# Attention weights two items ahead in second halves too, with scores for three items in the room of the eleventh gather slot

## What is computed

```python
def peer_ffn(xn, w_query, sub_keys, peer_u, peer_v):
    ...
    sk = jnp.einsum('thcd,ckd->thck', q, sub_keys).astype(jnp.float32)
    top_s, top_i = lax.top_k(sk, PEER_TOPK)
    ...
    best_s, best_pos = lax.top_k(cand_s, PEER_TOPK)
    idx = jnp.take_along_axis(cand_i, best_pos, axis=-1)
    gate = jax.nn.softmax(best_s, axis=-1)
    ...
        h = jnp.einsum('thkd,td->thk', peer_u[ib], xb).astype(jnp.float32)
        a = (gb * jax.nn.gelu(h, approximate=False)).astype(xb.dtype)
        return jnp.einsum('thk,thkd->td', a, peer_v[ib])
```

```python
    mx = jnp.maximum(jnp.max(sc, axis=-1, keepdims=True), sink)
    e = jnp.exp(sc - mx)
    pr = e / (jnp.sum(e, axis=-1, keepdims=True) + jnp.exp(sink - mx))
    ...
        a = jax.nn.softmax(sc, axis=-1)
        w = a[:, :, 0] - lam * a[:, :, 1]
```

## Time and profile before

| | us |
|---|---|
| median of 3 runs (2913.78 to 2915.91) | 2914.38 |
| the profiled execution | 2912.42 |
| its span, first to last instruction | 2910.6 |
| busy: PE, DVE, ACT, POOL | 2077.9, 2052.5, 1063.6, 1203.3 |
| mean granted TensorE clock | 0.850 |

### The profile page before, as it was taken

The page is one execution under the profiler, slowest core; times in us unless marked ns, Lnnn a source line. Parts: engine busy times, 40 slices in busy tenths (PEclk is TensorE's granted clock), DMA queues, the critical chain, the costliest instruction groups (busy, mean ns, idle before and its releaser), DMA issues.

```text
span 2910.6 us, 37403 instructions
## 1 busy us (share of the span) xinstructions
PE 2077.9 (71%) x12792; PEld 1031.8 (35%) x12792; DVE 2052.5 (71%) x5222; ACT 1063.6 (37%) x3372; POOL 1203.3 (41%) x1028
## 2 busy tenths in 40 slices
PE   8987887777868776677776877776776556555655
PEld 7644443344434432243442533224343111111111
DVE  3565678976667788866658678976657766677665
ACT  3432445623233456323224345633323222222222
POOL 0043343553344445444343444553444444444443
PEclk9998898888888888798887988888888776877687
DMA  6299999999999999999999999999999999999998
GB/s 236 105 422 420 421 421 397 406 419 419 421 421 420 421 421 414 417 421 421 421 420 382 421 421 421 421 418 421 421 420 418 420 419 417 419 418 416 417 417 333
DMA packets 162175, 1173.27 MB, mean 403 GB/s; under 512 B 17984, under 2 KB 18240, under 8 KB 19904
## 3 DMA queue, kind: packets, MB, share of 16 engines
q0 software_dynamic: 147456, 1073.81, 89.1%
q1 hardware_dynamic: 14528, 97.07, 8.2%
HBM read 1168.71 MB, written 2.10 MB: 402 GB/s over the span
## 4 chain that ended last, share of the span: by engine, by line
DMA 53%; PE 21%; DVE 18%; issue 4%; ACT 4%; POOL 0%; SPq 0%; DVEq 0%; POOLq 0%; ACTq 0%
DMA gather<-experts,idx 53%; PE ysum L810 10%; DVE gather L1513 9%; PE bank L533 7%; ACT amp L1089 2%; ACT diag L1097 1%; PE bank L584 1%; ACT gel L1082 1%; DVE shared L1242 1%; PE bank L610 1%; PE bank L555 1%; PE bank L779 1%; PE ysum L542 0%; DVE scratch L1438 0%; DVE scratch L1442 0%
## 5 line engine op out<-in xcount | busy, mean ns | idle before, releaser
L479 POOL DMA_INDIRECT gather<-experts,idx x1024 | 1203.1, 1175 | 1684.3 <-PE ysum L810 1323.2
L810 PE MATMUL ysum<-gather,diag 64*64 64x512 f32 x8192 | 1242.9, 758 | 717.0 <-ACT diag L1097 715.8
L1513 DVE CUSTOM_DVE_ANT_0 gather<-gather,xc 128x1024 f32<-128x1024 f32 x1024 | 1230.0, 1224 | 685.6 <-DMA gather<-experts,idx 647.6
L810 PEld LDWEIGHTS ysum<-gather,diag 64*64 64x64 f32 x8192 | 362.3, 170 | 1501.5 <-ACT diag L1097 925.9
L1082 ACT ACTIVATE gel<-hdot 128x4 f32<-128x4 f32 x255 | 52.4, 205 | 1588.8 <-DVE hdot L1513 1578.5
L533 PE MATMUL bank<-xnT,w 128*128 128x256 f32 (+1 forms) x2048 | 464.0, 382 | 11.2 <-DVE xnT L1167 11.2
L533 PEld LDWEIGHTS bank<-xnT,w 128*128 128x128 f32 x2048 | 377.8, 193 | 102.2 <-issue 40.8
L1097 ACT ACTIVATE diag<-cc,amp 128x64 f32<-128x64 f32 x1020 | 269.1, 333 | 8.6 <-PE ysum L810 4.4
L1089 ACT ACTIVATE amp<-gel,gate 128x1 f32<-128x1 f32 x1020 | 216.9, 283 | 8.4
L1082 ACT ACT_TABLE_LOAD x109 | 139.8, 1283 | 1.9
L779 PEld LDWEIGHTS bank<-w,yT 128*128 128x128 f32 x768 | 87.3, 192 | 17.4 <-issue 16.6
(11 more groups left out here) (151 smaller groups left out, 1486.2 us busy)
## 6 DMA issues: line engine op xcount, KB each, us to landing
w<-weights SPq DMA_DIRECT2D x82, 1024.0 KB
gather<-experts,idx POOLq DMA_INDIRECT x1024
gather<-weights SPq DMA_DIRECT2D x4, 1024.0 KB, 6.9
y_out<-x SPq DMA_DIRECT2D x4, 512.0 KB
x<-x_in SPq DMA_DIRECT2D x2, 512.0 KB, 4.4
g2b<-g_rows SPq DMA_DIRECT2D x2, 512.0 KB, 12.6
x<-x_in SPq DMA_DIRECT2D x1, 1024.0 KB, 13.3
cc<-consts_in SPq DMA_DIRECT2D x1, 856.0 KB, 11.0
```

What stands on the lines that cost most here:

```text
L479: pool.indirect_dma_start(gather[:, n % SLOTS, :], None, uv_d[m // 2], bass.IndirectOffsetOnAxis(ap=idx[:, g % 2, k:k + 1], axis=0)).then_ ...
L810: mm = nc.tensor.matmul(ysum[outs, q * 512:(q + 1) * 512], diag[toks, n % NDIAG, :], gather[toks, n % SLOTS, DM + hf * 512:DM + (hf + 1) * ...
L1513: e = V.tensor_tensor_reduce(out=gather[:, n % SLOTS, 0:DM], in0=gather[:, n % SLOTS, 0:DM], in1=xc[:, :], scale=1.0, scalar=0.0, op0=ALU. ...
```

## The change

Second halves hold the scores of three items. DVE makes the weights two items ahead of their turn, and ACT's exponential of item a + 2 moves from the end of slice a to its head. The copies in `pt` stay at two buffers (`TURNED`). The tile `shared` grows by 1024 floats a partition, and `gather` shrinks by one slot of 2048.

```diff
@@ -35,7 +35,7 @@
 HEADS, TOPK, NKEYS = 8, 16, 128
 CH = 4
 CHUNKS = HEADS * TT * TOPK // CH
-SLOTS = 11
+SLOTS = 10
 NDIAG = 4
 WS = 4
 BIG = 3.0e38
@@ -47,7 +47,8 @@
 ZP, ZH, ZG, ZC = (7, 8), (9, 12), (10, 13), (11, 14)
 NZ = 15
 NV = 3
-AHEAD = (4, 2)
+AHEAD = (4, 3)
+TURNED = (4, 2)
 
 Plan = namedtuple("Plan", "before z means conv pool squares sums")
 
@@ -232,10 +233,11 @@
         x = sb("x", SEQ // P, DM)
         gather = sb("gather", SLOTS, 2 * DM)
         xnT = sb("xnT", KD, HALF)
-        shared = sb("shared", 16 * HALF + 512)
+        shared = sb("shared", 16 * HALF + 1536)
         zt = shared[:, 0:10 * HALF].rearrange("p (i t) -> p i t", t=HALF)
 
-        sc = [shared[:, 10 * HALF:10 * HALF + 2048].rearrange("p (s m k) -> p s m k", s=n, m=2) for n in AHEAD]
+        sc = [shared[:, 10 * HALF:10 * HALF + 1024 * (2 + half)].rearrange("p (s m k) -> p s m k", s=n, m=2)
+              for half, n in enumerate(AHEAD)]
         qT = shared[:, 0:16 * HALF].rearrange("p (i t) -> p i t", t=HALF)
         kB = sb("kB", SEQ)
         kD = sb("kD", 2, SEQ)
@@ -257,7 +259,7 @@
         sq_y = xnT
         sd = sb("sd", 2, HALF)
         pt_all = sb("pt", 1024)
-        pt = [pt_all[:, :].rearrange("p (s k) -> p s k", s=n) for n in AHEAD]
+        pt = [pt_all[:, :].rearrange("p (s k) -> p s k", s=n) for n in TURNED]
         ss = sb("ss", 4)
         sdv = sb("sdv", 4)
         r1 = sb("r1", TT)
@@ -628,7 +630,7 @@
                 n = t + 1 - k0
                 for b in range(n):
                     mm = nc.tensor.matmul(ps[rows, 0:P], vAll[:, k0 + b, col:col + 64],
-                                          ptb[:, a % ahead, b * P:(b + 1) * P], start=b == 0, stop=b == n - 1)
+                                          ptb[:, a % TURNED[half], b * P:(b + 1) * P], start=b == 0, stop=b == n - 1)
                 mm.then_inc(s_ready, 1)
 
             def pool_product():
@@ -932,7 +934,7 @@
             def empty_turned(a):
                 swa, t, h, k0 = item(m, a)
                 cols = (t + 1 - k0) * P
-                empty(("t", a), ptb[:, a % ahead, 0:cols], bank_of(m, ("t", a))[:, 0:cols])
+                empty(("t", a), ptb[:, a % TURNED[half], 0:cols], bank_of(m, ("t", a))[:, 0:cols])
 
             def empty_out(a):
                 swa, t, h, k0 = item(m, a)
@@ -941,7 +943,7 @@
                       bank_of(m, ("o", a))[rows, 0:P])
 
             tile = [slice(t * P, (t + 1) * P) for t in range(TT)]
-            for a in range(ahead - 1 + half):
+            for a in range(ahead - 1):
                 attn_exp(a)
             for i in plan.before[1:]:
                 empty_z(i)
@@ -950,7 +952,7 @@
                 yield
             for a in range(ITEMS + 1 if m else plan.sums):
                 if a < ITEMS:
-                    if half == 0 and a + ahead - 1 < (ITEMS if m else 12):
+                    if a + ahead - 1 < (ITEMS if m else 12):
                         attn_exp(a + ahead - 1)
                     empty_turned(a)
                 if a:
@@ -965,9 +967,6 @@
                 if m:
                     if a == plan.sums:
                         root(("ys", 0), 3 * m + 1)
-                    if half and a + ahead < ITEMS:
-
-                        attn_exp(a + ahead)
                     yield
             if m:
                 root(("ys", 1), 3 * m + 2)
@@ -1325,8 +1324,7 @@
             if m:
                 yield
             attn_weights(0)
-            if half == 0:
-                attn_weights(1)
+            attn_weights(1)
             if m:
                 yield
             for a in range(ITEMS + 1 if m else plan.sums):
@@ -1340,9 +1338,9 @@
                     pool_tile(plan.means.index(a))
                 if a in plan.conv:
                     conv_tile(plan.conv.index(a))
-                if half and a + 1 < ITEMS:
-
-                    attn_weights(a + 1)
+                if half and a + 2 < ITEMS:
+
+                    attn_weights(a + 2)
                 if m:
                     if a == plan.sums + 1:
                         reciprocal_root(("ys", 0), 3 * m + 1)
```

## The result

The changed kernel took 2931.86 us (median of 4 runs, 2929.06 to 2935.16) against 2914.82 us for the kernel before beside it: a ratio of 1.0057, 95% interval 1.0046 to 1.0069. It is 17 us slower, nearly three times the 0.2% that a measurement can tell.

A forecast was written before the change was run, and what follows sets the result against it. The prediction took the gathers (DMA) to bound the kernel. Terms +2.0, +1.7 and +0.5 sum to +4.2 us on the profiled 2912.42, so 2916.6; the median being 2.0 above, 2918.6 us, range 2911 to 2926.

The forecast's parts named there:

- this attention: Second half's attention in the first block's experts: DVE's lateness and the missing slot cost +2.0 us, bounds -4 to +5.0.
- the other second half: Third block's experts: DVE falls some 7 us behind, mostly carried by the ring; +0.5 us, bounds 0 and 5.
- the slot elsewhere: Places where the ring is nearly empty, 702.33 us (1.2) and 1582 us (0.5): +1.7 us, bounds 0 and 5.
- my 15 to 35: Both second halves: DVE's new waits for ACT's exponentials were to total 15 to 35 us.
- my +3.3, +4.4 - 1.4 and -1.6: First block: DVE's waits at chunks 34 and 35, less the bias already done, and chunk 36's weights already done.
- the 2.74 us of chunk 29: First block, chunk 29: DVE's 2.74 us stand for the scores of item 10 was to go.
- Nearer to 2 than to 6: Dips around 500 us in the kernel before: real loss nearer 2 us than the 5.8 us of missing bytes.
- the first rival: First block's attention: DVE hardly waits, the 5.8 us of missing bytes return, less 1.7 for the slot: 2910.3 us; chance 0.12.
- The third rival: Slot missed at four or five long POOL silences, DVE's 7 us in the other second half reach DMA: 2926.4; chance 0.23.

The follow-up runs named there:

- again: The changed kernel unedited, measured once more beside the experiments: 2932.16 us, ratio 1.0063 against the kernel before.
- slot10: The kernel before with 10 gather slots in place of 11, nothing else changed: 2920.74 us, ratio 1.0023.
- slot9: The kernel before with 9 gather slots in place of 11: 2938.24 us, ratio 1.0084.
- wait11: The kernel before, 11 slots, scores for two items, with ACT's exponential moved into the slice of its weights: 2925.47 us, ratio 1.0037.
- order11: The changed kernel with 11 gather slots, the third item's scores laid over spent key scores: 2920.23 us, ratio 1.0020 against the kernel before.
- early10: The changed kernel, ten slots, with the exponential of item a+3 at the end of slice a: 2918.69 us, ratio 1.0015 against the kernel before.
- late11: order11, but in slice a DVE forms the weights of a+1, as in the kernel before: 2913.92 us, ratio 0.9999 against the kernel before.
- early11: The changed kernel with the edits of early10 and order11 together: 2913.58 us, ratio 0.9994 against the kernel before.
- busy11: early11 with useless DVE additions ahead of the weights where the changed kernel waits: 2928.51 us, ratio 1.0045 against the kernel before.

## Why the prediction was wrong

I said 2918.6 us, 2911 to 2926; it is 2931.9. One sign that I had asked for is missing: 490 to 510 us was to be above 380 GB/s and reads 379 and 331. And one that I had named as proof of being wrong is there, a dip between 1820 and 1900 us. These are windows of the changed kernel, and then the one of 1820 to 1900 us before and after:

```profile
490.00:500.00 10.00, 6.14 (x24) 2.71 (x28) 9.38 (x33) 7.44 (x20) 0.78 (x1) 0.50 0.91 379
500.00:510.00 10.00, 5.79 (x36) 1.62 (x32) 9.93 (x18) 2.02 (x9) 5.10 (x5) 0.67 0.90 331
```

```profile
1820.00:1900.00 80.00, 54.08 (x362) 21.75 (x360) 73.54 (x193) 51.63 (x135) 44.01 (x33) 0.89 1.01 421
1820.00:1900.00 80.00, 51.20 (x317) 20.44 (x317) 63.73 (x156) 47.80 (x121) 34.10 (x30) 0.83 0.97 390
```

To see where time was lost, take the start of a chunk's first dot product in the timeline of each run and subtract the kernel before's. The table has this lateness in us, first for chunks of the first block's experts, then of the third's, from one profiled execution each, so one or two microseconds in it say nothing.

| | chunk 20 | chunk 34 | chunk 37 | chunk 44 | third block, chunk 8 | third block, chunk 40 |
|---|---|---|---|---|---|---|
| start in the kernel before | 376.1 | 544.0 | 571.2 | 634.6 | 1655.1 | 1996.1 |
| changed kernel | 2.2 | 1.0 | 6.4 | 9.0 | 14.4 | 19.5 |
| again | 2.9 | 1.3 | 6.8 | 9.1 | 14.6 | 18.8 |
| slot10 | 0.1 | -0.2 | -0.1 | 2.2 | 6.7 | 5.2 |
| slot9 | 8.1 | 8.5 | 8.5 | 12.9 | 25.9 | 26.1 |
| wait11 | 2.0 | 2.1 | 10.2 | 10.7 | 10.8 | 14.8 |
| order11 | -0.1 | 0.2 | 5.6 | 6.1 | 4.4 | 7.8 |
| early10 | 3.5 | 1.3 | -1.7 | 3.3 | 7.7 | 6.7 |
| late11 | -1.7 | -0.5 | -1.7 | 0.2 | -0.4 | 0.1 |
| early11 | 1.1 | 0.6 | -2.4 | 1.4 | 1.3 | 1.6 |
| busy11 | 1.5 | 2.5 | 8.7 | 10.8 | 11.2 | 17.0 |

The mechanisms of the forecast were there, and all three terms of its sum were too small: this attention 2.0, measured 6.8 (chunk 20 to 44); the other second half 0.5, measured 5.1 (its chunk 8 to 40); the slot elsewhere 1.7, measured 5.4 between the two stretches and 2.2 up to chunk 20 (slot10 has 0.1 there, so the 2.2 are not safely the slot's).

**What came right.** 560 to 600 us was to be slower and is, and the waits of VectorE were found at their places and sizes. I had 3.3, 2.9, 2.6, 3.3 and 4.4 us in chunks 22, 23, 27, 34 and 35. The trace has 3.30, 2.96, 2.72, 3.51 and 4.60, out of the 0.01 us between table load and exponential that the row of before showed. The Trainium skill, ScalarE: Activation LUTs, section What ACT_TABLE_LOAD costs, adds a drain of 1380 ns to each switch. The trace disagrees: the load starts where the diagonals end, the exponential starts 0.02 us behind the load of 1.28 (562.97, then 564.27), and the waits fit without a drain. The total was 41.4 us, above my 15 to 35: from 1815 us on the third block has 14.6 us of waits where I had 12.6, but it has 9.4 us more in four waits before that, which I had not looked at. It also came right that the waits of chunks 22 to 27 are free: order11 stands 0.2 us late at chunk 34.

**The other second half, "+0.5", bounds 0 to 5: the step that failed by the largest factor.** The changed kernel lost 5.1 us there, ten times the term, and order11 3.4. I had VectorE 7 us behind by my own sum and let the ring carry that, because it had carried most of a silence of POOL of 17.93 us. But that was one silence behind a stretch with spare time. Here eight waits come within 260 us. The first four, up to 1806 us, cost no rate (421 GB/s from 1740 to 1820 us in both kernels). VectorE's waits from 1768 to 1932 us, of the kernel before and then of the changed one:

```profile
DVE gather L1513 <- DMA gather<-experts,idx: 14.8, 12, 3.4
```

```profile
DVE st L1263 <- ACT shared L915: 19.2, 6, 4.6
```

The changed kernel's VectorE has no wait for a gather left in these 164 us: its spare time there is used up, and at the last waits the rate falls (390 GB/s from 1820 to 1900 us). slot10 and early10 keep 418 GB/s in the window from 1810 to 1960 us and lose nothing between the two chunks of the table, order11 has 396. So the loss comes with the wait. Whether ten slots made it dearer (5.1 against 3.4 us) is not shown.

**This attention, "+2.0", bounds -4 to +5.** It lost 6.8 us, over its upper bound, and order11, with the slot in place, lost 6.2. I had VectorE 2.5 us late from chunk 36 on. order11 is 5.6 us late at chunk 37, and the way there can be followed. The waits of chunks 34 and 35 were paid as I had priced them (0.2 to 5.6 us; my +3.3, +4.4 - 1.4 and -1.6 make 4.7). What did not come is the gain ahead of them: by my sum VectorE was to be 2.2 us early at chunk 34. It came to chunk 29 1.2 us late (early11, without any of the waits, 1.4), was 1.7 us early at chunk 30, so the 2.74 us of chunk 29 did go, and lost that again in chunk 31, where its wait for scores grew from 3.2 to 4.67 us and I had +0.3. PE, too, was to be free 3.5 us earlier at chunk 29; it stands 7.91 us instead of 6.85, for a bank that the third item's scores need. I had read in the code that the six banks come in a fixed order, and had counted only the bank of item 10's scores. ScalarE's new order is the smaller part of that wait: early11, with the exponentials behind the copies, still has 6.70, and there ScalarE had stood 5.71 us for the chunk's dot products ahead of its copy. From chunk 37 to 44 the changed kernel loses 2.6 us more, about as slot10 does with 2.3, and order11 with its eleven slots 0.5: that is the slot.

**The slot elsewhere, "+1.7", bounds 0 to 5.** slot10 as a whole cost 7.1 us. At 700 us it lost 3.3 us more than before where I had 1.2, and 1.3 us in the window from 290 to 350, where I had nothing; at 1582 us, where I had 0.5, the stretch from 1560 to 1700 reads 401 GB/s in both. I had priced a slot as at most its own 2.49 us of transfer at a place; at 700 us the loss was more than that. In the table slot10, early10 and the changed kernel lose 4.5, 4.4 and 5.4 us between the two attention stretches, and order11, wait11 and early11 with their eleven slots nothing.

**"Nearer to 2 than to 6".** I held that the dips of before hid little loss. early11, which makes them shallower, gained 1.5 us with an interval that includes zero, so this stands as far as it was tested. From chunk 20 to 37 early11 gained 3.5 us on VectorE, and by chunk 44 nothing of it was left: VectorE waits for gathers again there, and they came no earlier. A gain as large as the first rival's was never there.

The third rival (2926.4, 0.23) had the mechanism nearest to what happened, the slot at several places and VectorE's lateness reaching DMA, and even its price was 5.5 us short. It had 5 us for the other second half, which is what was measured, and 5 for the slot's places; what it lacked is in this attention, where it kept my 2.0.

## What to carry to other kernels

When a consumer's step moves a slice earlier, move its producer's step too: here the exponential had stood a slice ahead of the weights, and keeping that distance gave back 12 of 17 us. Spare time covers a late step only at its own place: the four waits in chunks 22 to 27 fell on spare time and cost nothing, the two in chunks 34 and 35, 8.1 us, fell where there was none and left VectorE 5.4 us later. A forecast that sets a gain at one place against a wait at another must show that the gain is still there when the wait comes. The price of a slot in a ring of buffers was not a slope here: the eleventh slot was worth 7 us and the tenth 16. A slot given up for an optimisation is best priced by a run with one slot less, ahead of the optimisation.

## What the runs showed beyond that

The 16 DMA engines lost rate in windows in which their mean share stayed at 0.96 and 0.97 (480 to 620 us at 382 GB/s and 1810 to 1960 us at 394 in the changed kernel; full supply is 421 at 1.01): the loss is easier to see in GB/s than in the share.

TensorE's granted clock fell with the loss in the first stretch: from 560 to 600 us, 0.71 against 0.84 of full speed (2.4 GHz; the levels in between are mixtures with 1.2 GHz), with PE busy 25.1 us of 40 against 30.2, and DMA at 367 GB/s against 415. But wait11 loses as much there at nearly the clock of before:

```profile
560.00:600.00 40.00, 22.68 (x147) 9.28 (x148) 34.77 (x87) 21.38 (x59) 13.82 (x12) 0.80 0.93 361
```

In the second stretch it reads 0.80 in the changed kernel (394 GB/s) and 0.80 in early11 too (420 GB/s). So the clock is not what took the rate.
